# A hybrid attention and MoE layer on one core: zeros written in pieces, gates moved in the attention tile, stick-breaking sums in two float32r passes, and a register loaded earlier

## The reference

```
mod = silu(c) @ w_ada + b_ada                   # six vectors: shift, scale, gate, twice
h = rms_norm(x) * (1 + scale1) + shift1
proj = h @ w_in                                 # q, k, v of both branches, 3072 columns
o_dil = dilated_attention(rope(norm(qa)), rope(norm(ka)), va)   # 3 groups of 4 heads
o_sb = stick_breaking_attention(qb, kb, vb)     # 4 heads
g_dil, g_sb = sigmoid(h @ w_branch_gate)        # 2 x 1024 columns
x = x + gate1 * ((g_dil * (o_dil @ w_dil) + g_sb * (o_sb @ w_sb)) @ w_out)
h2 = rms_norm(x) * (1 + scale2) + shift2
x = x + gate2 * hierarchical_moe(h2)            # 32 experts, each token to 2 of them
```

```
softplus = -log_sigmoid(-z), 0 where masked
between[q, s] = -(sum of softplus[q, s'] over s' > s)
a = exp(log_sigmoid(z) + between), 0 where masked
o = a @ v
```

## Time and profile before

| | |
|---|---|
| time, median of 3 runs | 978.58 us (977.16 to 982.1) |
| the profiled execution: its time, its span | 977.41 us, 975.5 us |
| busy: PE, PE weight loads, DVE, ACT, POOL | 890.4, 512.5, 477.3, 197.0, 138.0 us |
| mean granted TensorE clock | 0.978 of full speed |
| transfers | 275.02 MB, 282 GB/s over the span |

### The profile page before, as it was taken

How to read it: one execution, slowest core, us unless ns; L and a number is a source line. 1 busy time by engine, 2 the same in 40 slices (tenths; PEclk the granted TensorE clock), 3 DMA queues, 4 the chain that set the end, 5 groups by cost and what they waited for, 6 DMA issues and landing times.

```text
span 975.5 us, 11214 instructions
## 1 busy us (share of the span) xinstructions
PE 890.4 (91%) x4193; PEld 512.5 (53%) x4193; DVE 477.3 (49%) x773; ACT 197.0 (20%) x330; POOL 138.0 (14%) x168
## 2 busy tenths in 40 slices
PE   3687999998889999999989999999999998998885
PEld 2255678997677666478644344434444333333332
DVE  2440355626788766633464334443444334243546
ACT  3431143324343433222210000000000000000000
POOL 1000121301331311251200100000000000000110
PEclk9798999999999999999899999999999999999998
DMA  9897666100205020464669999999999999999995
GB/s 344 316 323 275 230 214 221 61 37 6 98 23 185 1 86 1 172 259 173 247 270 353 423 420 422 421 421 420 421 421 422 422 421 422 421 422 423 422 413 227
DMA packets 60076, 275.02 MB, mean 282 GB/s; under 512 B 8756, under 2 KB 21052, under 8 KB 31876
## 3 DMA queue, kind: packets, MB, share of 16 engines
q1 hardware_dynamic: 54772, 264.41, 68.0%
q0 software_dynamic: 3952, 9.19, 2.5%
q10 hardware_dynamic: 1312, 0.87, 0.4%
HBM read 263.71 MB, written 14.70 MB: 285 GB/s over the span
## 4 chain that ended last, share of the span: by engine, by line
PE 60%; SPq 17%; DMA 10%; DVE 6%; issue 4%; ACT 3%; DVEq 0%; POOL 0%; POOLq 0%; ACTq 0%
PE ps L697 21%; PE ps L1057 14%; SPq L430 13%; PE ps L1076 7%; PE ps L1033 4%; DMA arena<-in_w_expert_down 3%; DMA xn<-in_w_ada 3%; SPq L438 2%; PE ps L655 2%; PE ps L848 2%; SPq L385 2%; ACT xn L1292 1%; PE ps L881 1%; DMA arena<-y_rows 1%; PE ps L873 1%
## 5 line engine op out<-in xcount | busy, mean ns | idle before, releaser
L1057 PE MATMUL ps<-arena,hT 128*64 128x512 f32 x1024 | 229.0, 596 | 4.9 <-DMA arena<-in_w_expert_up 4.9
L1057 PEld LDWEIGHTS ps<-arena,hT 128*64 128x64 f32 x1024 | 69.8, 137 | 146.9 <-issue 132.0
L1076 PE MATMUL ps<-arena,hT 128*64 128x512 f32 x512 | 116.9, 598 | 15.1 <-DMA arena<-in_w_expert_down 14.1
L1934 DVE TENSOR_SCALAR hT<-hT 128x256 f32<-128x256 f32 x32 | 9.4, 293 | 228.6 <-ACT hT L1406 228.6
L697 PE MATMUL ps<-slot_r,xs_r 128*128 128x512 f32 x320 | 106.6, 405 | 0.4 <-issue 0.4
L697 PE MATMUL ps<-xs_r,slot_r 128*128 128x512 f32 x320 | 102.5, 402 | 2.9 <-DVE hT_r L1508 2.9
L697 PE MATMUL ps<-slot_r,hT_r 128*128 128x512 f32 x224 | 88.3, 394 | 0.0
L697 PEld LDWEIGHTS ps<-slot_r,xs_r 128*128 128x128 f32 x320 | 77.6, 263 | 11.4 <-issue 3.1
L1076 PEld LDWEIGHTS ps<-arena,hT 128*64 128x64 f32 x512 | 34.1, 136 | 77.1 <-issue 57.7
L697 PEld LDWEIGHTS ps<-xs_r,slot_r 128*128 128x128 f32 x320 | 59.0, 190 | 19.5 <-issue 6.7
L621 POOL COPY idx<-small 128x1 int32 (+1 forms) x32 | 6.8, 212 | 418.0 <-DVE hT L1956 400.1
(11 more groups left out here) (292 smaller groups left out, 1072.7 us busy)
## 6 DMA issues: line engine op xcount, KB each, us to landing
arena<-in_w_expert_gate SPq DMA_DIRECT2D x64, 1024.0 KB, 25.6
arena<-in_w_expert_up SPq DMA_DIRECT2D x64, 1024.0 KB, 26.9
arena<-in_w_expert_down SPq DMA_DIRECT2D x32, 2048.0 KB, 29.6
xn<-in_w_ada SPq DMA_DIRECT2D x16, 1024.0 KB, 4.8
arena<-in_w_in SPq DMA_DIRECT2D x12, 1024.0 KB, 7.8
arena<-in_w_ada SPq DMA_DIRECT2D x8, 1024.0 KB, 14.2
arena<-in_w_branch_gate SPq DMA_DIRECT2D x4, 2048.0 KB, 8.4
xs<-in_x SPq DMA_DIRECT2D x8, 512.0 KB, 8.6
```

What stands on the lines that cost most here:

```text
L1057: mm = pe.matmul(ps[64 * h:64 * h + 64, 2, :], xeT[:, xb, k, CAP * j:CAP * (j + 1)], w_gu(b)[:, :, k, 256 * h:256 * h + 256], start=(k == ...
L1076: mm = pe.matmul(ps[64 * h:64 * h + 64, 4, :], hhT[:, f % 2, 64 * (f // 2):64 * (f // 2) + 64], w_dn(b)[:, f, h * CH:(h + 1) * CH], start= ...
```

## The change

Four edits. **Zeros**: the one transfer of 4 MB that clears `y_rows` becomes eight of 0.5 MB, from partitions 64 to 127 of `grow`, issued two at a time in GpSimd's first four rotary steps; VectorE's wait for them moves from the second vector of `mod` to the third. **Gates**: in the attention tile, `gate_finish(s)` moves from the first to the last place in VectorE's step. **Suffix sums**: ScalarE copies the softplus to a float32r high part (`split_sp`, in the place of `lg1`), VectorE subtracts it to leave the low part (in place), and TensorE runs the ten matmuls twice in float32r, over the high and over the low part, starting on the high part. **Count**: TensorE and VectorE load the register with the count before their last experts instead of after them.

```diff
-            link(pool.memset(grow[:], 0.0))
-            pool.dma_start(y_rows.rearrange("(p r) n -> p r n", p=P),
-                           grow[:].unsqueeze(1).to_broadcast([P, 4 * SEQ // P, CH])).then_inc(zero_out, 16)
+            link(pool.memset(grow[64:128, :], 0.0))
+            def clear_rows(i):
+                pool.dma_start(y_rows[4 * SEQ // 8 * i:4 * SEQ // 8 * (i + 1), :].rearrange("(p r) n -> p r n", p=64),
+                               grow[64:128, :].unsqueeze(1).to_broadcast([64, 4 * SEQ // 8 // 64, CH])
+                               ).then_inc(zero_out, 16)
...
+                if m < 4:
+                    clear_rows(2 * m)
+                    clear_rows(2 * m + 1)
...
-                pe.wait_ge(sp_ok, h + 1)
-                for j in range(NT):
+                def sums(part, j):
                     for j2 in range(j, NT):
                         a = b * CH + SB_OFF[j] + (j2 - j) * P
-                        mm = pe.matmul(psf[:, a:a + SEQ - j2 * P], (tri if j2 == j else ones)[:],
-                                       sp_[:, SB_OFF[j2]:SB_OFF[j2] + SEQ - j2 * P],
-                                       start=(j2 == j), stop=(j2 == NT - 1), skip_group_check=True)
+                        mm = pe.matmul(psf[:, a:a + SEQ - j2 * P], (tri_r if j2 == j else ones_r)[:],
+                                       part[:, SB_OFF[j2]:SB_OFF[j2] + SEQ - j2 * P],
+                                       start=(part is sp_hi and j2 == j), stop=(part is sp_lo and j2 == NT - 1),
+                                       skip_group_check=True)
+                    return mm
+                pe.wait_ge(sphi_ok, h + 1)
+                for j in range(NT - 1):
+                    sums(sp_hi, j)
+                pe.wait_ge(sp_ok, 2 * h + 2)
+                for j in range(NT - 1):
+                    sums(sp_lo, j)
+                sums(sp_hi, NT - 1)
+                mm = sums(sp_lo, NT - 1)
                 mm.then_inc(sf_ps, 1)
...
+            def split_sp(h):
+                act.wait_ge(sp_ok, 2 * h + 1)
+                act.activation(sp_hi, sp_[:, 0:SB_COLS], ACT.Copy).then_inc(sphi_ok, 1)
...
             sb_logs(0)
             gate_exp_(9)
+            split_sp(0)
...
                     sb_logs(h + 1)
                     gate_exp_(10 + 2 * h)
+                    split_sp(h + 1)
                 if h in (1, 2):
                     split_hi(10, h - 1)
                 sb_store(h)
...
             for s in range(2 * NT):
-                gate_finish(s)
                 probs_store(s)
...
                 if s - 2 >= NT:
                     out_T(s - 2 - NT)
+                gate_finish(s)
...
+            def split_sp(h):
+                dve.wait_ge(sphi_ok, h + 1)
+                dve.tensor_tensor(sp_lo, sp_[:, 0:SB_COLS], sp_hi.bitcast(F32), ALU.subtract).then_inc(sp_ok, 1)
...
             sb_copy(0)
             sb_softplus(0)
+            split_sp(0)
             gate_finish(9)
             out_T(3)
...
                     sb_softplus(h + 1)
+                    split_sp(h + 1)
                     gate_finish(11 + 2 * h)
...
+            top = last_slot(dve)
             for e in range(NE - 3, NE):
                 silu_up(e)
```

More of the change, by code:

```diff
@@ L84, in hybrid_layer @@
                 nc.sbuf_tensor("hT", [P, KC, SEQ], F32) as hT, \
-                nc.sbuf_tensor("xn", [P, NT, D], F32) as xn:
+                nc.sbuf_tensor("xn", [P, NT, D], F32) as xn, \
+                nc.sbuf_tensor("ones", [P, P], F32) as ones, \
+                nc.sbuf_tensor("tri", [P, P], F32) as tri:
             pass
@@ L90, in hybrid_layer @@
         xn_r = sb("xn_r", [P, NT, D], F32R)
+        ones_r = sb("ones_r", [P, P], F32R)
+        tri_r = sb("tri_r", [P, P], F32R)
         ident = sb("ident", [P, P])
-        ones = sb("ones", [P, P])
         strict = sb("strict", [P, P])
-        tri = sb("tri", [P, P])
         small = sb("small", [P, 1168])
@@ L177, in hybrid_layer @@
         zs, lg1, sp_ = xnf[:, 0:1536], xnf[:, 1280:2816], xnf[:, 2560:4096]
+        sp_hi, sp_lo = (xn_r[:].rearrange("p t n -> p (t n)")[:, at:at + SB_COLS] for at in (1280, 2560))
+        one = ones_r[:].bitcast(F32)
         gate1b = arena[:, 5 * SLOT_W + 2 * KC * P:5 * SLOT_W + 2 * KC * P + D]
@@ L356, in hybrid_layer, with last_slot, more_rounds @@
         KEPT = 2
-        def more_rounds(eng, body, after=None):
+        def last_slot(eng):
             eng.wait_ge(tables_ok, 1)
-            top = eng.value_load(cnt_i[0:1, 0:1], min_val=0, max_val=SEQ - 1)
+            return eng.value_load(cnt_i[0:1, 0:1], min_val=0, max_val=SEQ - 1)
+        def more_rounds(eng, body, after=None, top=None):
+            top = last_slot(eng) if top is None else top
             with eng.If(top + 1 > CAP):
@@ L630, in store @@
                 ).then_inc(y_out, 16)
-            pool.wait_ge(zero_out, 16)
+            pool.wait_ge(zero_out, 16 * 8)
             store(0, 0)
@@ L649, in _ @@
         def _(pe):
-            pe.wait_ge(consts, 4)
+            pe.wait_ge(consts, 6)
             def ada(lhs_k, rhs, first, last):
@@ L918, in _ @@
             for j in range(2):
-                mm = pe.matmul(ps[:, 6 + j, :], ones[32 * j:32 * j + 1, :], grow[32 * j:32 * j + 1, :],
+                mm = pe.matmul(ps[:, 6 + j, :], one[32 * j:32 * j + 1, :], grow[32 * j:32 * j + 1, :],
                                start=True, stop=True)
@@ L927, in second_gate_and_bias @@
                     r = 64 + 32 * j
-                    mm = pe.matmul(ps[64 * j:64 * j + 64, 6, :], ones[r:r + 1, 0:64], grow[r:r + 1, :],
+                    mm = pe.matmul(ps[64 * j:64 * j + 64, 6, :], one[r:r + 1, 0:64], grow[r:r + 1, :],
                                    start=True, stop=True)
@@ L982, in _ @@
                     pe.wait_ge(b2w_ok, 1)
-                    pe.matmul(ps[:, 7, 64:64 + NG + NE], ones[0:1, :], br[:], start=True, stop=True).then_inc(b2w_ps, 1)
+                    pe.matmul(ps[:, 7, 64:64 + NG + NE], one[0:1, :], br[:], start=True, stop=True).then_inc(b2w_ps, 1)
                 if j == 1 and t >= 1:
@@ L1006, in _ @@
             for back in range(1, NT + 1):
-                mm = pe.matmul(ps[:, 5, back * NE:(NT + 1) * NE], ones[:], AA5[:, 0:(NT + 1 - back) * NE],
+                mm = pe.matmul(ps[:, 5, back * NE:(NT + 1) * NE], one[:], AA5[:, 0:(NT + 1 - back) * NE],
                                start=False, stop=(back == NT), skip_group_check=True)
@@ L1140, in _ @@
             transpose_hot()
+            top = last_slot(pe)
             expert(NE - 1, *at(NE - 1), 1, 1, NE // 2 - 1, at(NE - 2), more=False)
@@ L1188, in _ @@
             exp_and_ln()
+            act.wait_ge(consts, 4)
+            act.activation(ones_r[:], ones[:], ACT.Copy).then_inc(consts, 1)
+            act.activation(tri_r[:], tri[:], ACT.Copy).then_inc(consts, 1)
             act.wait_ge(c_ld, 16)
```

18 lines of the change are left out of this document (9 added, 9 removed).

## The result

The changed kernel takes 981.29 us (median of 19 runs, 978.77 to 985.22), the kernel before 978.58 (19 runs beside them, 977.01 to 982.41). The ratio is 1.0025, with a 95% interval of 1.0015 to 1.0036: slower by 2.7 us. That is inside the 0.5% that was called "no change" and 3 us above the forecast of 978.3, but the interval does not reach 1: the kernel is slower, where the terms had been forecast to cancel. The sum is near, but its terms are not all right, as the rows and the single edits show.

A forecast was written before the change was run, and what follows sets the result against it. The expert stage was taken to last as long as its bytes, so time won or lost before its first load moves the end. Terms -7.6 - 5.6 + 12.3 + 1.5 - 0.9 = -0.3 us gave 978.3; range 968 to 987.

The forecast's parts named there:

- no change: Whole kernel: a difference within 0.5% (4.9 us), about what a measurement can tell from none; given 0.50.
- Zeros, -7.6: Clearing `y_rows`: 11.1 us of stall near 64 to 80 us go, pieces at the rotary steps cost 3.5; net -7.6.
- In all 11.1 us, which go away: At 64 to 80 us: TensorE's waits on `w_ada` loads behind the 4 MB of zeros, and the low clock after.
- I take 3.5 us: Cost of the eight pieces at GpSimd's first four rotary steps, with 1.2 and 11.1 us as ends.
- `w_ada` waits over 8 us in all: Sign that the prediction is wrong; expected were waits of 2 to 5 us on loads where the rotary steps begin.
- the average share of 0.67: Transfers between about 115 and 145 us in the kernel before, read as 9.9 us free of 30.
- half a `w_in`, 2 MB and the next load need 10 us where 8.4 are there: Rotary steps: four pieces issued within some 2 us while a `w_in` half is under way, at 421 GB/s.
- the third rival: Pieces at the `w_ada` loads of units 9 to 13 take twice as long: 12.3 us lost, total +8.5, 987; chance 0.17.
- Gates, -5.6: Attention tile: steps 1 to 5 gain 8.5 us, steps 6 and 7 nothing, VectorE's order before the first softplus costs 2.9.
- Suffix, +12.3 and +1.5 for the clock: Heads: the split delays ScalarE, VectorE and GpSimd, values(3) +12.3 us; TensorE's lower clock adds 1.5; ends +5.5 and +17.
- I had put 6.8 less: First rival: port does not catch `gate_finish(13)` and `(15)`; suffix +5.5 instead of +12.3, total -7.1, 971.5; chance 0.18.
- Count, -0.9: VectorE's last path: register load moved ahead and hidden by waits for weights; -0.9 us, bounds -0.5 and -1.6.

## Why the prediction was right or wrong

**Zeros, -7.6: wrong.** "In all 11.1 us, which go away" held (11.2 measured where nothing takes their place). The step that failed is "I take 3.5 us" for the pieces. Measured were 9.7 in the kernel with this edit alone and, in the profiled execution of the changed kernel, 11.9 at the first negation: near or above the upper end of 11.1 that I had kept and given too little weight. By the prediction's own sign, "`w_ada` waits over 8 us in all", it was wrong: they sum to 9.3.

Two readings were behind the 3.5. The free time was read from the average share of 0.67, where six of the eight pieces meet 0.86 and 0.90. And I had written that half a `w_in`, 2 MB and the next load need 10 us where 8.4 are there, which is 1.6 for one such place. In the changed kernel the load issued at 110.13 needed 13.5 us, in which 4.8 MB moved at 359 GB/s, with a third pair of pieces issued behind it; and TensorE stood from 116.13 on, so that 6.0 were there. The difference is the wait of 7.5 (5.9 with the edit alone). The number of pieces at a time is part of it (one piece a step: 2.3), the 64 partitions hardly. The lower clock behind the wait had no term either: 0.52 for 10 us with 6.33 busy is about 3.0 us at the full clock's rate, an estimate from the window's row.

By the rule of the Trainium skill, "SBUF — State Buffer", section "Door 1: The DMA port swizzle (why `[64,N]` ≈ `[32,N]`)", transfers from partitions 64 to 127 get about half the bandwidth. What I made of it in the third rival, pieces that take twice as long, did not come: 8.9 against 8.7 us for the pieces, 26.0 against 22.7 for the 4 MB. That rival's price of 12.3 us is close to the 11.9, but not by its mechanism. The rule itself is not refuted: beside other loads the transfer from 128 partitions was slower too (22.7 us against 13.4 in the idle stretch), 26.0 is no more than twice 13.4, and no run here sends from 64 partitions with nothing beside it.

**Gates, -5.6: right in size, wrong on its own.** The softplus comes 6.5 us earlier alone and 6.6 in the changed kernel. The parts are less near than their sum: from the first negation to that of step 5 11.7 us are won (forecast 8.5), steps 6 and 7 lose 1.5 (22.9 us together, 21.4 before; forecast nothing), and from there to the softplus 3.4 are lost (forecast 2.9). And alone the edit gives 1.2, since the order of ScalarE and GpSimd at the first softplus was read from the kernel before and not walked again with the softplus 6 us earlier. In the changed kernel the suffix edit's copy happens to hold the weight split back.

**Suffix, +12.3 and +1.5 for the clock: right.** Alone +14.0. The walk through the heads held: the `tensor_scalar` of gates 13 and 15 took 3.63 and 3.89 us (forecast: waits of 3.4), and the last values product came 15.8 us later from the first softplus (forecast 12.3, and 1.5); with `z(1)` at the full clock, in the kernel with gates and suffix sums, it was 13.4. `sb_args(3)` came 14.4 later (forecast 14). What these two waits are worth was too low: without them I had put 6.8 less, and 10.9 less was measured. The lower clock behind TensorE's idle time is part of it (1.8 us in the last product). The pass was estimated at 2.9 us for both and took 3.2.

**Count, -0.9:** 0.87 in the profile, not distinguishable from nothing in the time.

**The sum** was -0.3 and came out as +2.7. The zeros and the count were forecast at -8.5, gave -2.9 as the sum of the two alone, and nothing on top of the other two edits (+2.7 with them, +2.6 without; the intervals leave room for 1 or 2 us either way). The gates and the suffix edit were forecast at +8.2 together and gave +2.6. Of this second difference the profiles show most: at the last values product the two edits stand at +5.6 (-7.7 at the first softplus, +13.4 from there), the experts' stage gives 1.2 back, and the rest is that the kernel before was profiled 1.9 below its median on that chip. So an error of 8.6 us and one of 5.6 partly cancel: that the forecast was near is luck.

## What to carry to other kernels

Walk an edit again with the other engines where it puts them: a step that comes 6 us earlier meets other operations at the shared port, and one wait on ScalarE (5.4 us here) or the order of two of its instructions (10.9 us) decides whether the gain stays. Read the free time of the transfers where a new one will be issued, and not as the average of the stage. Before splitting a transfer into pieces among loads that arrive just in time, look for a stretch with a DMA share near zero and put it there whole. A cheaper form of an instruction was worth nothing here, on an engine that waits for the work that the form needs.

## What the runs showed of the hardware

- TensorE's clock can take back part of what is won elsewhere, and not where the edit is. With one wait of 2.4 us it stayed at 1.00 in one kernel and fell to the 1.2 GHz level in another, and the attention stage, 214 to 320 us, ran at a mean of 0.98 before, 0.92 and 0.89 with two ways to place the zeros. Over 24 runs of the kernel before on one chip, a mean clock 0.01 lower went with 5.7 us more (correlation -0.77); on the three other chips, with 14 to 19 runs each, it was 2.8 to 3.7. What decides it, the rows don't tell.
- The lock between VectorE and GpSimd can chain. GpSimd's two subtractions back to back (9.25 us) held two short VectorE operations, 4.48 and 4.72 us: one got in between them, the other after. This agrees with the Trainium skill, "SBUF — State Buffer", section "Who interferes with whom".
- A 4 MB transfer took 13.4 us from issue to landing where the other transfers were idle, and 22.7 beside the `w_ada` loads. A `w_ada` load of 1 MB, 5.0 us in the median, took 13.5 with six pieces of 0.5 MB and a `w_in` load issued within 10 us around it.
